# Matmul operands of a two-block transformer kernel laid at multiples of 128 bytes in SBUF

## What is computed

```python
def reference(x, ...):
    x = first_block(x, ...)     # per layer: three mixers on slices of x @ w_in, then w_out;
                                # layer 0 a dense SwiGLU, layer 1 eight experts (top 2); a gated projection
    return second_block(x, ...)

def second_block(x, w_in, w_branch, w_gate, b_gate, w_o, ...):
    for l in range(DEPTH):                                   # DEPTH = 2
        x = x + 0.5 * swiglu_2(rms_norm_2(x, norm_g[l, 0]), ffn_w_gate[l, 0], ffn_w_up[l, 0], ffn_w_down[l, 0])
        h = rms_norm_2(x, norm_g[l, 1])
        proj = h @ w_in[l]                                   # 1024 x 3840, then three kinds of attention
        g = jax.nn.sigmoid(h @ w_gate[l] + b_gate[l])        # 1024 x 3072
        merged = sum(g[:, :, n] * (y[n] @ w_branch[l, n]) for n in range(3))
        x = x + merged @ w_o[l]
        x = x + 0.5 * swiglu_2(rms_norm_2(x, norm_g[l, 2]), ffn_w_gate[l, 1], ffn_w_up[l, 1], ffn_w_down[l, 1])
    return rms_norm_2(x, final_g)

def swiglu_2(h, w_gate, w_up, w_down):                       # 1024 -> 2816 -> 1024
    return (jax.nn.silu(h @ w_gate) * (h @ w_up)) @ w_down
```

## The kernel before

| stage | activations | high and low weights | apart |
|---|---|---|---|
| mixers of block 1 (L516) | 64 | 96 | 32 |
| gated projections (L516) | 0 | 32 | 32 |
| dense stage, block 1: L741, L747 | 0 | 64 | 64 |
| dense stage, block 1: L764 | 64 (`hid_hi`, `hid_lo`) | 64 | 0 |
| dense stages, block 2: L741, L747 | 96 | 32 | 64 |
| dense stages, block 2: L764 | 32 | 32 | 0 |
| mixers, block 2 (L2916, L2914, L2877) | 32 (also `branch_parts`) | 64 | 32 |
| experts (L2336, L2354) | 0 | 0 | 0 |

## Time and profile before

### The profile page before, as it was taken

One profiled execution on the slowest core, in us unless ns is written; L12 is line 12 of the kernel. 1 busy time (PEld: TensorE's weight loads), 2 busy tenths in 40 slices (PEclk: granted clock), 3 DMA queues, 4 the chain that ended last, 5 costly groups with the idle time before them and its releaser, 6 DMA issues. The chain is left out here.

```text
span 2833.5 us, 45742 instructions
## 1 busy us (share of the span) xinstructions
PE 2744.6 (97%) x17552; PEld 2317.3 (82%) x17552; DVE 2140.6 (76%) x3168; ACT 1568.5 (55%) x2445; POOL 21.6 (1%) x22
## 2 busy tenths in 40 slices
PE   8999999999999999999999999999999999999998
PEld 8848888857787787787778889988888888988887
DVE  7568767568899889889877776675877776666776
ACT  6254446256777777777765335554534434555533
POOL 0100000100000000000000000000000000000000
PEclk9999999999999999999999999999999999999999
DMA  6435443108879889889874556334454555245451
GB/s 261 141 126 208 184 153 115 64 20 345 344 312 375 330 326 376 325 336 364 332 289 179 180 191 183 137 120 171 181 202 154 206 188 197 86 162 191 166 199 39
DMA packets 102350, 599.26 MB, mean 211 GB/s; under 512 B 23212, under 2 KB 28844, under 8 KB 33080
## 3 DMA queue, kind: packets, MB, share of 16 engines
q1 hardware_dynamic: 102200, 597.18, 55.8%
HBM read 594.24 MB, written 6.12 MB: 212 GB/s over the span
## 5 line engine op out<-in xcount | busy, mean ns | idle before, releaser
L2458 DVE TENSOR_TENSOR expert_w_low<-weight_ring,expert_w_high 128x1024 fp32r<-128x1024 f32 x528 | 630.5, 1222 | 62.8 <-ACT expert_w_high L2404 52.0
L2404 ACT ACTIVATE expert_w_high<-weight_ring 128x1024 fp32r<-128x1024 f32 x528 | 555.2, 1059 | 102.8 <-PE psum L2336 55.2
L741 PE MATMUL psum<-hnT_parts,weight_high 128*128 128x512 f32 x1680 | 410.0, 394 | 0.0
L799 DVE TENSOR_TENSOR weight_low<-weight_ring,weight_high 128x1024 fp32r<-128x1024 f32 x330 | 385.1, 1218 | 7.0 <-ACT weight_high L793 7.0
L741 PEld LDWEIGHTS psum<-hnT_parts,weight_high 128*128 128x128 f32 x1680 | 313.6, 187 | 75.2
L793 ACT ACTIVATE weight_high<-weight_ring 128x1024 fp32r<-128x1024 f32 x330 | 326.1, 1048 | 7.8 <-PE psum L764 5.9
L812 ACT ACTIVATE gate_act<-gate_sum 128x256 f32<-128x256 f32 x110 | 46.0, 418 | 505.2 <-DVE gate_sum L862 505.1
L2336 PE MATMUL psum<-expert_w_high,expert_x_high 128*128 128x512 f32 x704 | 288.8, 410 | 1.8 <-DVE expert_x_low L2477 1.6
L2916 PE MATMUL psum<-hnT_parts,slab_high 128*128 128x256 f32 x1440 | 278.4, 288 | 0.0
L2336 PE MATMUL psum<-expert_w_high,expert_x_low 128*128 128x512 f32 x704 | 276.3, 392 | 0.0
L2336 PE MATMUL psum<-expert_w_low,expert_x_high 128*128 128x512 f32 x704 | 274.9, 390 | 0.0
(11 more groups left out here) (418 smaller groups left out, 4852.4 us busy)
## 6 DMA issues: line engine op xcount, KB each, us to landing
weight_ring<-in_moe_w SPq DMA_DIRECT2D x264, 1024.0 KB, 6.8
weight_ring<-in_w_in SPq DMA_DIRECT2D x52, 1024.0 KB, 6.2
weight_ring<-in_ffn_w_gate SPq DMA_DIRECT2D x44, 1024.0 KB, 4.8
weight_ring<-in_ffn_w_up SPq DMA_DIRECT2D x44, 1024.0 KB, 6.4
weight_ring<-in_ffn_w_down SPq DMA_DIRECT2D x44, 1024.0 KB, 4.8
weight_ring<-in_ffn_w SPq DMA_DIRECT2D x33, 1024.0 KB, 4.8
weight_ring<-in_w_gate SPq DMA_DIRECT2D x24, 1024.0 KB, 4.7
weight_ring<-in_w_branch SPq DMA_DIRECT2D x24, 512.0 KB, 3.5
```

What stands on the lines that cost most here:

```text
L741: nc.tensor.matmul(sums(t, k), hi[:, kt, :], hn[2][:, kt, :, :], start=(kt == 0), stop=(kt == KT - 1), skip_group_check=True)
L799: nc.vector.tensor_tensor(lo, raw, as_f(hi), ALU.subtract).then_inc(split_lo.sem, 1)
L2404: nc.scalar.activation(part(0, k, half), raw(c, k, half), ACT.Copy).then_inc(high[k].sem, 1)
L2458: nc.vector.tensor_tensor(part(1, k, half), raw(c, k, half), as_f(part(0, k, half)), ALU.subtract).then_inc(low[k].sem, 1)
```

## The change

The two helpers that take buffers get an alignment. `tmp` has a new argument, 32 bytes unless told otherwise, and these buffers are asked for at 128: the slab parts of `SplitSlabs`, `hid_hi`, `hid_lo`, `weight_high` and `weight_low` of the dense stage, `hnT_parts` everywhere, and `qkT`, the first of block 2's mixer. In that mixer the other operands come to multiples of 128 by order: `lam` and `sink` go behind `branch_parts`, and the norm's small buffers and `half_bias` behind the slab parts, the gates and the softmax buffers.

As built, every buffer named in the table above lies at a remainder of 0 after the change, and the distances are all 0. The expert stage's buffers don't move. Sizes are the same; the buffers end at most 160 bytes later. The instructions of each engine, their order, their waits and their shapes are the same in both kernels: only addresses differ.

```diff
@@ class Core
-    def tmp(self, ctx, name, shape, dt=F32):
+    def tmp(self, ctx, name, shape, dt=F32, align=32):
 
         self.count += 1
-        return ctx.enter_context(self.nc.sbuf_tensor(f"{name}_{self.count}", shape, dt))
+        return ctx.enter_context(self.nc.sbuf_tensor(f"{name}_{self.count}", shape, dt, align_bytes=align))
@@ class SplitSlabs
-        self.parts = [K.tmp(ctx, n, [P, slots, SLAB], F32R) for n in ("slab_high", "slab_low")]
+        self.parts = [K.tmp(ctx, n, [P, slots, SLAB], F32R, align=128) for n in ("slab_high", "slab_low")]
@@ def dense_ffn_stage
-        hid_hi = K.tmp(ctx, "hid_hi", [P, 3, SEQ], F32R)
-        hid_lo = K.tmp(ctx, "hid_lo", [P, 3, SEQ], F32R)
-        high = K.tmp(ctx, "weight_high", [P, 2, 3, KT * P], F32R)
-        low = K.tmp(ctx, "weight_low", [P, 2, 3, KT * P], F32R)
+        hid_hi = K.tmp(ctx, "hid_hi", [P, 3, SEQ], F32R, align=128)
+        hid_lo = K.tmp(ctx, "hid_lo", [P, 3, SEQ], F32R, align=128)
+        high = K.tmp(ctx, "weight_high", [P, 2, 3, KT * P], F32R, align=128)
+        low = K.tmp(ctx, "weight_low", [P, 2, 3, KT * P], F32R, align=128)
@@ class Block2Tensors
-        self.qkT = sb("qkT", [P, 22, SEQ])
+        self.qkT = K.tmp(ctx, "qkT", [P, 22, SEQ], align=128)
...
+        parts = sb("branch_parts", [P, 2, 4, SEQ], F32R)
         self.lam = sb("lam", [P, 4])
         self.sink = sb("sink", [P, 8])
-        parts = sb("branch_parts", [P, 2, 4, SEQ], F32R)
@@ def mixer_stage
         hn = hn_parts(K, ctx)
+        high, low = (sb(n, [P, PIECE_SLOTS, SLAB // 2], F32R) for n in ("slab_high", "slab_low"))
+        gate = sb("branch_gate", [P, 3, 2, SEQ])
+        logit, prob, probT = sb("logit", [P, 2, 2, SEQ]), sb("prob", [P, NP, 2, SEQ]), sb("probT", [P, NPT, 4, P])
         norm = NormTurn(K, ctx, vec_at(VEC2, "norm_g_2", layer) + KT, K.cols2, NORM_BANKS, hn)
-        high, low = (sb(n, [P, PIECE_SLOTS, SLAB // 2], F32R) for n in ("slab_high", "slab_low"))
-        gate, half_bias = sb("branch_gate", [P, 3, 2, SEQ]), sb("half_bias", [P, 24])
-        logit, prob, probT = sb("logit", [P, 2, 2, SEQ]), sb("prob", [P, NP, 2, SEQ]), sb("probT", [P, NPT, 4, P])
+        half_bias = sb("half_bias", [P, 24])
@@ def hn_parts
-    both = K.tmp(ctx, "hnT_parts", [P, KT, 2, SEQ], F32R)
+    both = K.tmp(ctx, "hnT_parts", [P, KT, 2, SEQ], F32R, align=128)
```

## The result

| | before | after |
|---|---|---|
| median, us | 2833.45 (6 runs) | 2844.43 (6 runs) |
| lowest to highest | 2829.31 to 2840.33 | 2842.38 to 2846.64 |
| span of the profiled execution | 2833.5 | 2840.6 |

The ratio of after to before is 1.0039, with a 95% interval from 1.0027 to 1.0051: the changed kernel is 11 us slower, where 26 us less had been forecast. The time lies above the forecast range, which ended at 2840, and within the 0.5% called no change.

The account below looks back on a forecast made before the run. TensorE, busy 97% of the span, was taken as the bound; 11.2 + 20.7 + 1.3 - 5.9 = 27.3 us saved, taken as 26, from a median of 2835.0 gave 2809 us, range 2798 to 2840.

Parts of the forecast that it names:

- L2336 against L2877: Experts' product against block 2 mixer's output product: one form, 226.7 against 233.3 ns, so the operands' distance was held to decide.
- The table of distances: Operand distances before the change: 64 for L741 and L747, 0 for L764 and experts, 32 for L2877; all 0 after.
- Term 1: Dense stages, L741: 1680 matmuls from 233.4 to 226.7 ns, 11.2 us saved.
- Term 2: Mixers' 256-column products L2916, L516 and L2914: 4608 matmuls gain 4.5 ns each, 20.7 us saved.
- Term 3: Output product of block 2's mixer, L2877: 192 matmuls gain 6.6 ns each, 1.3 us saved.
- term 4: Starts of runs in L741 and the 256-column products stay above the floor: 297 x 0.02, 5.9 us not saved.
- Term 5: Dense stages, L747 and L764: at or near the floor, nothing taken; 8.4 us lost if L747 fell to L2916's cost.
- Terms 6 and 7: VectorE, ScalarE and loads don't see the place and don't become the bound; experts' 825 us unchanged.
- Slower: Rival, chance 0.06: distance 0 good for 512 columns, bad for 256 in L747 and the mixers; 18.9 us more, 2854.
- point of decision: Slower decides once a 256-column matmul at distance 0 costs 2 ns more than now, from 12.5 us / 6288.
- The clock: Granted clock read from the profile page as at its upper level, 2.4 GHz, in all 40 slices.
- The rule on SBUF: Skill's page against the forecast: TensorE's two reads are independent, so distance could cost nothing and the sum would be 0.

Follow-up runs that it names:

- The scans: Three runs of the changed kernel, dense-stage weight parts 0 to 448 bytes from the activations in 32-byte steps, slab parts moved too: 2841.0, 2844.7 and 2843.8 us.
- scan_d: Changed kernel with both operands moved in two dense stages, high and low parts at different distances in two others and in the mixers: 2834.4 us.
- scan_a: Changed kernel with weight parts 0, 32, 64, 96 and 128 bytes from the activations in the five dense stages, slab parts moved too: 2841.0 us.

## Why the prediction was wrong

- **That the distance of TensorE's two operands counts, and not the place: right, though not the whole.** The scans and scan_d bear it out; the distances of the neighbouring matmuls count too. The argument came from L2336 against L2877, and L2877 did what it said.
- **The table of distances: wrong, and the first step to fail.** I took remainders modulo 128. The period is 256, so the dense stages went from 64 to 128, not to 0, and so did the products of block 1, from 32 or 224. Term 1, 11.2 us for L741, came to 0.8.
- **Term 2, 20.7 us for 4608 products of 256 columns: wrong in sign, +6.2.** The prediction said that no row shows a 256-column product at remainder 0, and took L747's 113.7 and half of the experts' 226.7 as its price. L2917 had a true distance of 0 and 120.0 ns. The rows nearest in form were far in the one thing that mattered, the distance at half the length. What is best for 512 columns is near the worst for 256.
- **Term 3, 1.3 us for L2877: right**, 1.0 measured, with a start of some ten matmuls ahead of the floor, as term 4 had it. (In L741 at a true 0 there is no such start to see: 226.9 ns over the whole stage in scan_a, so term 4's 5.9 us were too much; nothing hung on it here.)
- **Term 5, nothing for L747 and L764: wrong.** Its own alternative, 8.4 us if L747 fell to L2916's cost, is what happened, 8.0; L764 added 1.8, though its distance stayed 0. L747 at 114 ns with a distance of 64 was listed as what "don't fit so well". It was the row to follow: a 256-column product at the floor at 64, beside others at 118 at 32, said that 256 columns had a good distance of their own, and that the change would move them off it.
- **Terms 6 and 7, the other engines and the experts: right.** VectorE's durations are the same, L2336 and L2354 within 0.1 ns.
- **The rivals.** "Slower" named the mechanism, good for 512 and bad for 256, and had a chance of 0.06. Its L747 term held (8.4 against 8.0), but by luck, since L747 came to lie at 128 and not at 0; the mixers lost 6.2 us and not 23.0; and the 12.5 that it gave back for L741 and L2877 were 1.8. So it said 18.9 where the steps give 14.2 and the medians 11.0. Its 6288 products of 256 columns lost 8.0 + 6.2 = 14.2 us, 2.3 ns each, just past its point of decision of 2 ns; with only 1.8 us given back the true point was at 0.3. Even a true distance of 0 in the dense stages would have brought little: by the scan 1680 x (233.3 - 226.9) = 10.8 us less for L741 and 1680 x (119.5 - 114.1) = 9.1 more for L747, 1.7 us in sum and before L764; no run has all three at 0.
- **The clock.** "At its upper level in all 40 slices" read a 9 as full; the mean was 0.986. The sum does not use it, but it is worth as much as some of its terms: 0.004 of mean clock between two executions is some 8 us.
- **The range** ended at 2840 because it stood on the chance of 0.06 for all that is slower. Distances of two reads that hinder each other can go either way, and nothing but the missing row spoke for this one.
- **The rule on SBUF.** Step times that move from 226.9 to 233.8 ns and from 113.5 to 120.1 by addresses alone, with both operands TensorE's own, speak against what the Trainium skill says in SBUF — State Buffer, section Who interferes with whom, that TensorE's two reads are independent and it never waits on anyone: the measurement decides, and what the places of the two operands cost together is not nothing. Its section Operand start alignment speaks of what is legal and not of speed; the runs show that a legal address can cost up to 6% of a 256-column product's time (120.1 against 113.5 ns). What in the hardware has the period I did not find. That the two reads meet is argued from the distance; no run here separates the load's own read from that of the matmul beside it.

## What to carry to other kernels

Before buffers are aligned, tabulate the full distance of stationary from moving operand for each form of matmul beside its step in the timeline, and treat the forms that are at their floor as what a change can lose. For fp32r products here the stationary operand 64 bytes below the moving one (192 modulo 256) was best in the dense stages, with their mix of 512 and 256 columns, the pair (64, 192) for the high and the low slab in the mixers, and 0 only for 512 columns alone. Two kernels whose sums differ by 10 us are better compared at the same mean granted clock than by their medians. Choose whole patterns that a run has shown together, since the best value of each form, taken singly, did not combine.

## What the runs showed of the hardware that I had not expected

- The step of an fp32r matmul depends on the distance of its operands with a period of 256 bytes: 512 columns 226.9 to 233.8 ns, 256 columns 113.8 to 120.1 in the scans, the same within 0.05 ns one period on, in steps of 32 bytes; finer places, 16 or 4 bytes off, have values of their own.
- In the dense stages distance 0 is the best for L741's 512 columns (226.9) and near the worst for L747's 256 (119.5); 192 is the one good for both (230.1 and 113.8), while the mixers' 256-column products had 117.8 there.
- The sign counts: 192 and 64 gave L741 230.1 and 232.9.
- The step is not a matter of a matmul's own distance alone. L747 at distance 64 took 114.1 ns in every row of sixteen or 114.1 and 117.8 by turns, by where L764's operands lay; with its high part elsewhere it took 117.7 at a distance at which it takes 113.5.
- Executions of one kernel differ by about 2 us of 2833 for each 0.001 of mean granted clock (2827.5 us at 0.991, 2849.0 at 0.982).
- The floor of an fp32r product was 226.7 ns for 512 columns and 113.3 for 256, 17/16 of the 213.3 and 106.7 that one column in each period of 2.4 GHz would make; not one form went below it over a stage.
